# The end of a two-block model in one kernel: merge in banks, fused norms, a small product moved between other work, stores by tile

## The reference, cut to what matters

```python
merged = jax.nn.sigmoid(g_att) * y_att + jax.nn.sigmoid(g_gla) * y_gla      # y_gla = (...) @ w_branch_gla
h = h + merged @ w_out[l]
h = h + expert_choice_ffn(rmsnorm_2(h, norm_ffn[l]), w_router[l], w_exp_gate[l], w_exp_up[l], w_exp_down[l])
ple_gate = jax.nn.sigmoid(rmsnorm_2(h, norm_ple[l]) @ w_ple_gate[l])
h = h + ple_gate * (p[l] @ w_ple[l])                                          # p: 512 x 256, w_ple: 256 x 1024
return rmsnorm_2(h, norm_final)
```

## Time and profile before

| | |
|---|---|
| median of 3 runs | 2269.45 us (2267.28 to 2272.2) |
| the profiled execution's own time | 2269.2 us |
| its span | 2267.4 us |
| PE busy | 2007.2 us, 89% |
| POOL busy | 1034.3 us, 46% |
| DVE busy | 783.5 us, 35% |
| ACT busy | 521.8 us, 23% |
| bytes moved by DMA | 330.66 MB, mean 146 GB/s |

### The profile page before, as it was taken

One profiled execution on the slowest core, in us unless ns is written; L12 is line 12 of the kernel. 1 busy time (PEld: TensorE's weight loads), 2 busy tenths in 40 slices (PEclk: granted clock), 3 DMA queues, 4 the chain that ended last, 5 costly groups with the idle time before them and its releaser, 6 DMA issues.

```text
span 2267.4 us, 23351 instructions
## 1 busy us (share of the span) xinstructions
PE 2007.2 (89%) x9426; PEld 1458.4 (64%) x9426; DVE 783.5 (35%) x1178; ACT 521.8 (23%) x1075; POOL 1034.3 (46%) x604
## 2 busy tenths in 40 slices
PE   4988898979999999997899989976869999999875
PEld 3877786667778888886667568864644444444353
DVE  3254558442322302325344445534131111111122
ACT  2434436322421101102222413420100000000021
POOL 4696766736367878875544475444400000000041
PEclk9999998999999999998999899988969999999988
DMA  4320112312122333332211132112359999999821
GB/s 123 95 82 29 38 47 93 121 47 84 56 75 85 101 94 95 101 93 87 65 56 47 47 84 57 56 49 100 137 233 409 409 409 409 409 409 409 354 93 47
DMA packets 115269, 330.66 MB, mean 146 GB/s; under 512 B 7223, under 2 KB 8459, under 8 KB 115163
## 3 DMA queue, kind: packets, MB, share of 16 engines
q1 hardware_dynamic: 111808, 318.79, 39.4%
q0 software_dynamic: 1760, 5.05, 0.7%
q10 hardware_dynamic: 1594, 5.32, 0.7%
HBM read 324.94 MB, written 4.19 MB: 145 GB/s over the span
## 4 chain that ended last, share of the span: by engine, by line
PE 75%; DVE 7%; POOL 6%; DMA 4%; ACT 4%; issue 2%; POOLq 1%; ACTq 0%; DVEq 0%; SPq 0%
PE bank L549 46%; PE bank L1694 11%; PE bank L1724 3%; PE bank L1711 3%; POOL shared_r L573 2%; PE bank L711 2%; DMA shared<-in_w_exp_gate 2%; DMA arena<-in_w_exp_gate 2%; POOL shared_r L574 2%; POOLq L188 1%; PE bank L1366 1%; POOL shared_r L592 1%; DMA arena<-in_w_exp_down 1%; PE bank L446 1%; PE bank L1379 1%
## 5 line engine op out<-in xcount | busy, mean ns | idle before, releaser
L549 PE MATMUL bank<-shared_r 128*128 128x512 f32 (+1 forms) x4032 | 965.0, 396 | 67.3 <-POOL shared_r L574 25.2
L549 PEld LDWEIGHTS bank<-shared_r 128*128 128x128 f32 x4032 | 748.0, 195 | 246.1 <-issue 56.8
L573 POOL TENSOR_TENSOR shared_r<-shared,small 128x1024 fp32r<-128x1024 f32 (+1 forms) x184 | 355.8, 1933 | 488.5 <-PE bank L549 471.7
L574 POOL TENSOR_TENSOR shared_r<-shared,shared_r 128x1024 fp32r<-128x1024 f32 (+1 forms) x184 | 454.4, 2469 | 14.5
L1964 POOL DMA_DIRECT2D arena<-in_p x1 | 0.8, 758 | 520.5 <-DVEq L188 520.5
L1694 PE MATMUL bank<-shared,arena 128*64 128x512 f32 x880 | 194.9, 594 | 8.2 <-issue 3.4
L549 PE MATMUL bank<-shared_r,arena_r 128*128 128x512 f32 x768 | 176.1, 391 | 0.0
L549 PEld LDWEIGHTS bank<-shared_r,arena_r 128*128 128x128 f32 x768 | 144.2, 188 | 31.5
L1694 PE MATMUL bank<-arena 128*64 128x512 f32 x656 | 145.7, 594 | 9.1 <-DMA arena<-in_w_exp_gate 3.5
L1694 PEld LDWEIGHTS bank<-shared,arena 128*64 128x64 f32 x880 | 69.5, 137 | 127.6 <-issue 127.0
L1773 DVE TENSOR_TENSOR X<-bank,X 128x512 f32<-128x512 f32 x64 | 44.3, 692 | 240.8 <-PE bank L1711 240.8
(11 more groups left out here) (395 smaller groups left out, 2097.9 us busy)
## 6 DMA issues: line engine op xcount, KB each, us to landing
shared<-in_w_in SPq DMA_DIRECT2D x80, 512.0 KB, 3.6
shared<-in_w_exp_gate SPq DMA_DIRECT2D x38, 1024.0 KB, 18.5
shared<-in_w_exp_up SPq DMA_DIRECT2D x36, 1024.0 KB, 18.6
shared<-in_w_exp_down SPq DMA_DIRECT2D x36, 1024.0 KB, 18.6
arena<-in_w_exp_up SPq DMA_DIRECT2D x28, 1024.0 KB, 18.6
arena<-in_w_exp_down SPq DMA_DIRECT2D x28, 1024.0 KB, 18.6
arena<-in_w_exp_gate SPq DMA_DIRECT2D x26, 1024.0 KB, 18.6
shared<-in_w_up SPq DMA_DIRECT2D x32, 512.0 KB, 3.7
```

Source lines behind the costliest of these rows:

```text
L549: ins = pe.matmul(dst, W_, x_, start=first, stop=final)
L573: link(pool.tensor_tensor(hi, raw(p), small[:, 18:19].to_broadcast([P, hi.shape[1]]), ALU.add))
L574: pool.tensor_tensor(lo, raw(p), hi.bitcast(F32), ALU.subtract).then_inc(S_("w_split"), 1)
```

## The change

The meetings behind `proj_r` are gone, and their place is taken by waits on banks and named semaphores.

- Merge in banks: DVE multiplies a bank of `ygla` by the sigmoid and adds MERGED, both in the bank; ACT copies the high half from there, DVE subtracts the low half. `ygla` and `out2` run with `ready`. ACT, not POOL, issues the reload of X, and also p, `w_ple`, the router's weights and the last gain.
- `out2` is planned as two halves with the transposes of p between them.
- The product of p and `w_ple` (`ple_product`, eight banks) moves from the end: three banks between `out2` and n6's transposes, two behind the router, three behind the affinities' transposes. ACT evacuates them, writes 2 MB to `p_keep` in DRAM, and waits for it before the first expert. SP reads them back into `PP` when PE has done the last up product, and then loads the parts of `ple_gate`.
- n6 and n7 are fused norms; n6's transposes are evacuated by ACT and DVE in turn. The router, the affinities and the slots use one bank each.
- The ring's slots are ordered anew: the first six in `arena`, issued once `ygla` is merged and the parts of `out2` have been issued; two when `out2` is done; the rest when the router is.
- The end: squares of half tiles behind the additions, the gain multiplied by DVE beside it for two tiles, which ACT then scales, while DVE does the other two in one operation each; four stores, one for each tile.

```diff
-          ("ygla", 8), ("out2", 8), ("norm_ffn", KT), ("router", 4), ("affT", 4), ("slotT", 4), ("experts", 19 * PAIRS),
-          ("norm_ple", KT), ("ple_gate", 8), ("turn_p", 2), ("ple", 8)]
+          ("ygla", 8), ("out2a", 4, LEFT), ("turn_p", 2, (6, 7)), ("out2b", 4, RIGHT), ("ple_a", 3, (0, 1, 2)),
+          ("norm_ffn", KT, RIGHT), ("router", 1, (3,)), ("ple_b", 2, (0, 1)), ("affT", 1, (4,)), ("ple_c", 3, (5, 6, 7)),
+          ("slotT", 1, (2,)), ("experts", 19 * PAIRS), ("norm_ple", KT), ("ple_gate", 8)]
...
+    p_keep = nc.dram_tensor("p_keep", (P, 8 * 512), F32, kind="Internal").ap()
...
-    stage("out2", A["w_out_2"], (0, 512))
+    PB["out2"] = len(panels)
+    add(A["w_out_2"], 0, 512, BASE["out2a"])
+    add(A["w_out_2"], 512, 512, BASE["out2b"])
...
-    FUSED = ("n2", "n4", "n5")
+    FUSED = ("n2", "n4", "n5", "n6", "n7")
...
-                bank_done(act, added + i * ST + j)
+                bank_done(act, added[i * ST + j])
...
+        if whole:
+            for d in range(0, KT, 2):
+                bank = bank_take(act, base + d)
+                bank_release(act.activation(dst[:, d, :], bank[:, :], ACT.Copy, scale=par(gain, d)), base + d)
+            return
...
+    def fused_dve(dve, link, tag, added, gain, dst, base, whole=False):
...
+        dve.wait_ge(S_("fused_sq"), fth(tag) - (tag in ("n6", "n7")))
         dve.tensor_tensor(var[:, 0], mean8[:, 0, 0], mean8[:, 0, 1], ALU.add).then_inc(S_("fused_ms"), 1)
...
+        if whole:
+            for d in range(1, KT, 2):
+                bank = bank_take(dve, base + d)
+                bank_release(dve.tensor_scalar(dst[:, d, :], bank[:, :], par(gain, d), None, ALU.mult), base + d)
+            return
...
+    ring_at = a.at
+    ring = [a.take(XPANEL) for _ in range(6)]
+    ring += [shared[:, i * XPANEL:(i + 1) * XPANEL] for i in (2, 3, 0, 1, 4, 5, 6, 7)]
...
+    PIN = AOH[0].rearrange("p a s -> p (a s)").rearrange("p (j d) -> p j d", j=ST)
+    PTT = AOH[1]
+    PS_ = [arena[:, hg_at + 512 * i:hg_at + 512 * i + 512] for i in range(6)] + [bc[:, 512 * i:512 * i + 512] for i in range(2)]
+    PP = arena[:, ring_at:ring_at + ST * D].rearrange("p (i j d) -> p i j d", i=2, j=ST)
...
+    def ple_product(pe, g):
+
+        bank = bank_claim(pe, ple[g])
+        for k in range(2):
+            ins = pe.matmul(bank[:, :], PTT[:, k, g % ST * P:(g % ST + 1) * P], WP[:, k, g // ST * 512:g // ST * 512 + 512], start=k == 0, stop=k == 1)
+        bank_ready(ins, ple[g])
+
+    def ple_evacuate(act, g):
+
+        bank = bank_take(act, ple[g])
+        bank_release(act.activation(PS_[g], bank[:, :], ACT.Copy), ple[g])
...
-        early("ygla")
-        meet()
-        rest("ygla")
-        early("out2")
-        bank_done(pool, BASE["ygla"] + 7)
-        pool.wait_ge(S_("x_kept"), 16)
-        pool.dma_start(X[:, :, :], x_keep.rearrange("(j p) d -> p j d", p=P)).then_inc(S_("x_back"), 16)
-        meet()
-        rest("out2")
-        pool.wait_ge(S_("x_back"), 16)
-        meet()
...
-        meet()
-        pool.dma_start(PIN[:, :, :], A["p_2"][0].rearrange("a (j p) d -> p (a j) d", p=P)).then_inc(S_("p_in"), 16)
-        pool.wait_ge(S_("p_in"), 16)
-        meet()
+        rest("ygla", 0)
+        rest("out2", 0)
         rest("ple_gate", 0)
...
         gla_turn(pe, 1)
-        meet()
         for i in range(2):
-            product(pe, PB["ygla"] + i, [GTS[:, b] for b in range(2)], fm=True)
-        meet()
-        pe.wait_ge(S_("merged"), 1)
-        for i in range(2):
-            product(pe, PB["out2"] + i, XB, fm=False)
-        meet()
-        ends["out2"] = meet.n
-        norm_pe(pe, "n6", ST, BASE["norm_ffn"])
...
-        ends["router"] = meet.n
-        expert_gather(pe, 0)
-        for i in range(PAIRS):
...
-        meet()
-        ends["experts"] = meet.n
-        norm_pe(pe, "n7", ST, BASE["norm_ple"])
-        meet()
-        for i in range(2):
-            product(pe, PB["ple_gate"] + i, XB, fm=False)
+            product(pe, PB["ygla"] + i, [GTS[:, b] for b in range(2)], fm=True, ready=eight("turn_gla"))
+        product(pe, PB["out2"], XB, fm=False, ready=eight("ygla"))
+        pe.wait_ge(S_("p_in"), 16)
...
+        product(pe, PB["out2"] + 1, XB, fm=False)
+        for k in range(2):
+            bank_done(pe, BASE["turn_p"] + k)
+        pe.wait_ge(S_("wp_in"), 16)
+        for g in range(3):
+            ple_product(pe, g)
+        fused_pe(pe, "n6", BASE["norm_ffn"])
+        pe.wait_ge(S_("wr_in"), 16)
+        n = BASE["router"]
+        bank = bank_claim(pe, n)
+        for j in range(ST):
+            for k in range(KT):
+                if j == 0:
+                    bank_done(pe, BASE["norm_ffn"] + k)
+                ins = pe.matmul(bank[:, j * NE:(j + 1) * NE], XT[:, k, j * P:(j + 1) * P], WR[:, k, :], start=(k == 0), stop=(k == KT - 1))
+        bank_ready(ins, n)
+        for g in range(3, 5):
+            ple_product(pe, g)
...
+        for g in range(5, 8):
+            ple_product(pe, g)
+        pe.wait_ge(S_("slt"), 1)
...
+        expert_gather(pe, 0)
+        for i in range(PAIRS):
+            expert_pe(pe, i)
+        bank_done(pe, x_bank["o", PAIRS - 1, 0])
+        expert_scatter(pe, PAIRS - 1)
+        fused_pe(pe, "n7", BASE["norm_ple"])
+        for i in range(2):
+            product(pe, PB["ple_gate"] + i, XB, fm=False, ready=eight("norm_ple"))
...
-        meet()
         act.activation(SGG, SGG, ACT.Sigmoid).then_inc(S_("sgg"), 1)
-        meet()
-        for i in range(2):
-            act.activation(XTS[:, 0, 4 * i:4 * i + 4, :], MERGED[:, 4 * i:4 * i + 4, :], ACT.Copy).then_inc(S_("mg_hi"), 1)
-        meet()
-        norm_act(act, "n6", X, ST, "norm_ffn_2", XT, BASE["norm_ffn"], whole=True)
...
         for i in range(8):
-            n = BASE["ple_gate"] + i
-            bank = bank_take(act, n)
-            bank_release(act.activation(PG[:, i % 4, i // 4 * 512:i // 4 * 512 + 512], bank[:, :], ACT.Sigmoid), n)
+            n = BASE["ygla"] + i
+            act.wait_ge(S_("y_sum"), i + 1)
+            act.activation(XTS[:, 0, i, :], banks[BANK[n]][:, :], ACT.Copy).then_inc(S_("y_hi"), 1)
+        act.dma_start(X[:, :, :], x_keep.rearrange("(j p) d -> p j d", p=P)).then_inc(S_("x_back"), 16)
+        act.dma_start(PIN[:, :, :], A["p_2"][0].rearrange("a (j p) d -> p (a j) d", p=P)).then_inc(S_("p_in"), 16)
+        act.dma_start(WP[:, :, :], A["w_ple_2"][0].rearrange("(k p) n -> p k n", p=P)).then_inc(S_("wp_in"), 16)
+        act.dma_start(WR[:, :, :], A["w_router_2"][0].rearrange("(k p) n -> p k n", p=P)).then_inc(S_("wr_in"), 16)
+        act.dma_start(bc[:, D:2 * D], A["norm_final_2"].partition_broadcast(P)).then_inc(S_("gain_in"), 16)
...
+        fused_act(act, "n6", out2, "norm_ffn_2", XT, BASE["norm_ffn"], whole=True)
+        for g in range(3):
+            ple_evacuate(act, g)
+        act.wait_ge(S_("rmax"), 1)
+        act.activation(AFF[:, :, :], AFF[:, :, :], ACT.Exp).then_inc(S_("rexp"), 1)
+        for g in range(3, 8):
+            ple_evacuate(act, g)
+        act.drain().then_inc(S_("p_out"), 1)
+        act.wait_ge(S_("p_out"), 1)
+        act.dma_start(p_keep[:, 0:6 * 512], arena[:, hg_at:hg_at + 6 * 512]).then_inc(S_("p_kept"), 16)
+        act.dma_start(p_keep[:, 6 * 512:8 * 512], bc[:, 0:D]).then_inc(S_("p_kept"), 16)
+        act.wait_ge(S_("p_kept"), 32)
+        for i in range(PAIRS):
+            expert_act(act, i)
+        fused_act(act, "n7", last_scatter, "norm_ple_2", XTS, BASE["norm_ple"])
+        for i in range(2):
+            for j in range(ST):
+                n = BASE["ple_gate"] + ST * i + j
+                bank = bank_take(act, n)
+                bank_release(act.activation(half(PG, j, i), bank[:, :], ACT.Sigmoid), n)
+            if i:
+                act.activation(small[:, 19:20], eps_, ACT.Sqrt)
+            for j in range(ST):
+                act.wait_ge(S_("x_ple"), i * ST + j + 1)
+                last = act.activation(SQF[:, i, j, :], half(X, j, i), ACT.Square, scale=1.0 / 32.0, accum_out=mean8[:, 0, i, j:j + 1])
+        last.then_inc(S_("end_sq"), 1)
+        act.wait_ge(S_("end_ms"), 1)
+        act.activation(var[:, 0], var[:, 0], ACT.Sqrt, bias=eps_).then_inc(S_("end_sd"), 1)
+        act.wait_ge(S_("end_r"), 1)
+        for j in range(2):
+            act.activation(X[:, j, :], XS[:, j, :], ACT.Copy, scale=inv[:, 0, j:j + 1]).then_inc(S_("y_act"), 1)
...
         dve.wait_ge(S_("sgg"), 1)
-        for i in range(8):
-            n = BASE["ygla"] + i
-            bank = bank_take(dve, n)
-            release_own(dve, dve.tensor_tensor(TMP[:, i, :], bank[:, :], SGG[:, i, :], ALU.mult), n)
-            dve.tensor_tensor(MERGED[:, i, :], MERGED[:, i, :], TMP[:, i, :], ALU.add)
-        meet()
-        for i in range(2):
-            dve.wait_ge(S_("mg_hi"), i + 1)
-            last = dve.tensor_tensor(XTS[:, 1, 4 * i:4 * i + 4, :], MERGED[:, 4 * i:4 * i + 4, :], XTS[:, 0, 4 * i:4 * i + 4, :].bitcast(F32), ALU.subtract)
```

(63 more changed lines are left out.)

167 lines of the change are left out of this document (38 added, 129 removed).

## The result

The changed kernel takes 2196.82 us (median of 4 runs, 2194.61 to 2198.18) against 2269.3 for the kernel before (4 runs, 2267.28 to 2272.2): a ratio of 0.9679, interval 0.9662 to 0.9696. The profiled execution has a span of 2195.2 against 2267.4, so 72.2 us are gone where 68.6 were forecast.

A forecast was written before the change was run, and what follows sets the result against it. It took TensorE or waits for it as the bound, with weights a second candidate in the experts. Gains of 30.5 in front, 10.6, 1.8 and 25.7 behind sum to 68.6, from 2269.2 to 2200.6 us; range 2190 to 2214.

The forecast's parts named there:

- to the end of `out2`: From `ygla`'s start through `out2`: earlier start 1.6, hole closed 21.3, faster product 1.9, less 0.9 for p's transposes; gain 23.9 us.
- n6 and router: From `out2`'s end to the router's end: six moved products 5.2, transposes 3.5, router 10.8; 19.5 against 27.1, gain 7.6 us.
- The merge: Between `ygla` and `out2`: tiles finished in banks under `out2`'s first parts, so the hole goes; gain 21.3 us.
- n7: Between last scatter and `ple_gate`: 5.6 us to the transposes and 6.3 for them, 11.9 against 22.5; gain 10.6.
- merge in the open: Rival in front of `out2`: the merge must be complete first, 5 to 8 us come back, 2207; chance 0.06.
- The router: The router's 32 products behind n6: 10.8 us taken again, with the clock falling; 6.4 if all at full clock.
- the clock stays: Rival from `out2` to the gather: 2.4 GHz throughout because moved products fill the holes, 2191.9 us; chance 0.15.
- The four products behind the router: Moved products ahead of the affinities' transposes: 5.2 us at a middle clock, a loss of 2.0.
- The rival of late panels: Panels or late transfers miss their first use; 20 to 35 us late gives 2207 to 2222; chance 0.10.
- that of a lower clock there: Rival in the experts: the chip grants TensorE less clock, slower than before below 0.84, 2300 at 0.80; chance 0.04.
- The tail: From `ple_gate`'s end to the span's end: last tile done at 8.6, end at 12.8 against 38.5; gain 25.7 us.
- The moved product: Second product leaves the end, 16 x 0.89 = 14 us gone there; its first six products take 5.2 before n6's transposes.

The follow-up runs named there:

- Experiment 1: The changed kernel, but TensorE waits for all eight merged tiles before it starts the `out2` product; 2209.02 us, ratio 0.9733.
- experiment 3: The changed kernel with the merge through SBUF tiles, and ScalarE issuing the load of p ahead of the last three high halves and X's reload; 2200.71 us.
- experiment 2: The changed kernel with the merge's product and sum going through tiles in SBUF instead of the bank, same order and waits; 2207.53 us, ratio 0.9722.
- experiment 4: The changed kernel with the first six moved products put behind the affinities' transposes instead of ahead of n6's transposes; 2195.67 us, ratio 0.9672.
- experiment 6: The changed kernel with the product of p and `w_ple` back behind `ple_gate`, p's transposes behind n7's, and no `p_keep`; 2211.76 us, ratio 0.9746.
- experiment 5: The changed kernel with the four moved products behind the router put behind the affinities' transposes instead; 2194.83 us, ratio 0.9668.
- experiment 7: The changed kernel, but SyncE holds expert panels 9 to 14 until the first one-hot matrix is ready; 2199.66 us, ratio 0.9694.
- experiment 8: The changed kernel, but GpSimd's second split of `ple_gate` waits for n7's scalings of the first tile; 2196.27 us, ratio 0.9675.

## Why the prediction was right, step by step

The forecast was 2200.6 and the median is 2196.82. The first gather starts at 1639.08 (forecast near 1643), the last scatter ends at 2126.55 (near 2130.5). By stretches of the chain, the gains forecast and measured:

| stretch | forecast | measured |
|---|---|---|
| to the end of `out2` | 23.9 | 25.2 (1624.52 to 1599.32) |
| n6 and router | 7.6 | 9.95 (27.08 to 17.13) |
| router to gather | -1.0 | -0.6 (22.02 to 22.63) |
| gather to last scatter's end | 0 | -0.1 |
| scatter to `ple_gate` | 10.6 | 11.5 (22.53 to 11.01) |
| `ple_gate` product | 1.8 | 1.5 (45.37 to 43.86) |
| its end to the end of the span | 25.7 | 24.7 (38.5 to 13.8) |
| sum | 68.6 | 72.2 |

The sum came 3.6 short: terms too small by 5.0 together, terms too large by 1.4. So the total is near for the right reason in the main, and only 1.4 us of it is errors that cancel.

- **The merge** is hidden as forecast: the bank operations take 0.68 to 0.70 beside GpSimd's splits. Experiment 1 shows what the order of the parts does: without it a hole of 4.8 is left. The other 16.5 of the 21.3 go with the rest of the edit, and the chain before says with what. GpSimd's drain in the meeting waited for its own reload of X, and ScalarE and VectorE then split the tiles after it:

```profile
1562.93 9.41 POOLq L188
1572.37 1.92 ACT shared_r L2249
...
1574.38 4.51 DVE shared_r L2447 x2
```

That reading is the chain's alone; no experiment puts the meeting or the reload back. Two statements of the prediction need an answer. "An operation that cost twice as much would still be covered to within a microsecond or two" holds for the tiles (1.0 lost in the first panel, experiment 3, with operations of up to 2.9), but not for the end, because the load of p hangs behind the merge on ScalarE's queue (experiment 2). And the rival "merge in the open" was priced at 5 to 8; a hole of 4.8 cost 10.
- **To the end of `out2`** 1.2 of the 1.3 more lie in the `ygla` product, which the forecast left as it was: 45.5 instead of 46.7. It starts at 0.50 in both kernels, and the clock is back at about 1511 instead of 1514.5.
- **The router** is the mis-sized term: I took 10.8 "again", and it took 8.48. It was the rival "the clock stays" in part, which I had left out of the sum. The six products in front are not enough to explain it. Without them it takes 8.94 (experiment 4), or 11.04 where p's transposes are gone too (experiment 6); with them it takes 8.48, but 9.36 to 9.61 in experiments 1 to 3, where TensorE had waited for tiles or for p more than 30 us before. What differs is how long the clock holds from the router's start, worked out from the granted clock over the router's whole length: 5.4 us in the changed kernel, 4.8 and 2.6 in experiments 4 and 6, 4.0 to 4.3 in experiments 1 to 3, 3.5 before the change. Moving the six products is worth 0.5 of the 2.3; what sets the rest stays open.
- **n6's transposes** (5.15 and 3.49, forecast 5.2 and 3.5) came to the tenth, the six products first and at full clock.
- **The four products behind the router** took 5.43, forecast 5.2. That they could as well have stood behind the affinities is worth 3.2 at the gather (experiment 5), a cost that the forecast knew as 2.0 (5.2 less 3.2) net.
- **The experts** moved as a block, and neither the held panels nor 2 MB each way mattered much (1.3 us in experiment 7, 1.0 at most in experiment 6). The rival of late panels is refuted by experiment 7, and that of a lower clock there by the changed kernel's rows: the clock is 1.00 from 1700 to 2119.
- **n7** took 11.0 instead of 11.9: 5.7 to the transposes (forecast 5.6) and 5.3 for them (6.3). The 5.7 are in part luck. In the earlier trace rows one scaling lost 1.6 to GpSimd's splits; here no scaling did, but an addition of four columns took 2.3 of it. The 1.0 in the transposes is the clock (experiment 8).
- **The tail** took 13.8 instead of 12.8. The last tile is done at 2189.53, 8.1 behind the product (forecast 8.6), though a gain multiplication of 0.6 stands ahead of the reciprocal in VectorE's order. From there to the end are 5.7, against 4.2: the store and what follows it are the term that was too small (the four stores took 2.7 to 4.8 to land; 3.7 was assumed for the last). The table load was 1.28 again, and the operation behind it started 0.01 later. The Trainium skill (ScalarE: Activation LUTs, "Table sets: the hidden batching unit") has 2.7; this case's rows decide.
- The moved product is worth 12 to 15 us of the 72: 14.9 in the medians (experiment 6), of which 2.8 belong to the order of sigmoids and squares there. Its terms in the forecast were 14 gained at the end and 4.0 lost in front: 0.9 for p's transposes, 1.1 for the six products (5.2 instead of 4.1) and 2.0 for the four. In front it cost 1.2, as without it the clock falls sooner.

Open: what sets the moment at which the clock falls in the router and comes back in n7's transposes (5.2 to 6.5 us), and where the untouched front's drift of a few microseconds comes from. Of the gains, those of the meetings alone and of the fused norms alone were not tried by themselves.

## What to carry to other kernels

Look for the hole in front of a product and for the order of its first parts: if they use only what has long been ready, a merge of 5 us disappears, and the clock stays up behind it, which in experiment 1 was worth as much again. Before calling an operation covered, list what its engine issues behind it, DMA issues above all. Work that has to be moved is best put where TensorE would idle ahead of something costly, and not where it merely stands in line ahead of a chain that others wait for.
